# One 512-column product for both halves of the activations in the loops of the feed-forward stages

## The reference

```python
def _swiglu(x, w_in, w_out):
    gate, up = jnp.split(x @ w_in, 2, axis=-1)
    return (jax.nn.silu(gate) * up) @ w_out
...
def swiglu(h, wg, wu, wd):
    return (jax.nn.silu(h @ wg) * (h @ wu)) @ wd
...
    h = x
    for i in range(DEPTH):                       # DEPTH = 1
        h = h + 0.5 * _swiglu(_rmsnorm(h, ffn1_norm[i]), ffn1_w_in[i], ffn1_w_out[i])
...                                              # mix
        h = h + 0.5 * _swiglu(_rmsnorm(h, ffn2_norm[i]), ffn2_w_in[i], ffn2_w_out[i])
...                                              # ple
    return _rmsnorm(h, final_norm)
...
    for i in range(DEPTH_2):                     # DEPTH_2 = 2
        mod = c_act @ ada_w[i] + ada_b[i]
        sh1, sc1, g1, sh2, sc2, g2, sh3, sc3, g3 = jnp.split(mod, N_MOD, axis=-1)
        h = modulate(rms_norm(x, ln_ffn1[i]), sh1, sc1)
        x = x + 0.5 * g1[:, None, :] * swiglu(h, ffn1_wg[i], ffn1_wu[i], ffn1_wd[i])
...                                              # attn where i is 0, sgu where i is 1
        h = modulate(rms_norm(x, ln_ffn2[i]), sh3, sc3)
        x = x + 0.5 * g3[:, None, :] * swiglu(h, ffn2_wg[i], ffn2_wu[i], ffn2_wd[i])
        x = rms_norm(x, ln_out[i])
```

## Time and profile before

| | us |
|---|---|
| median of 3 runs | 1601.67 |
| lowest and highest | 1601.16, 1603.94 |
| the profiled execution's own time | 1601.59 |
| its span in the profile | 1599.8 |

### The profile page before, as it was taken

One profiled execution on the slowest core, in us unless ns is written; L12 is line 12 of the kernel. 1 busy time (PEld: TensorE's weight loads), 2 busy tenths in 40 slices (PEclk: granted clock), 3 DMA queues, 4 the chain that ended last, 5 costly groups with the idle time before them and its releaser, 6 DMA issues.

```text
span 1599.8 us, 30197 instructions
## 1 busy us (share of the span) xinstructions
PE 1550.6 (97%) x12438; PEld 1510.9 (94%) x12438; DVE 1116.6 (70%) x1327; ACT 740.1 (46%) x823; POOL 13.0 (1%) x33
## 2 busy tenths in 40 slices
PE   6999999799999999999999899999999999999998
PEld 6999998689999999999888799999999999899998
DVE  4777879956887867877767677788644466654444
ACT  5433354354333574333567643335533346453333
POOL 1000000000000000000000000000000000000000
PEclk8999999899999999999999999999999999999999
DMA  6998854238888448888443388885555554545551
GB/s 212 344 313 295 285 158 154 84 126 283 295 290 309 162 152 301 308 304 296 138 158 115 106 299 304 294 279 196 182 184 184 184 158 151 166 159 184 184 184 53
DMA packets 244682, 341.08 MB, mean 213 GB/s; under 512 B 5891, under 2 KB 188315, under 8 KB 244624
## 3 DMA queue, kind: packets, MB, share of 16 engines
q1 hardware_dynamic: 242656, 334.72, 62.4%
q0 software_dynamic: 1968, 5.54, 0.9%
HBM read 339.17 MB, written 2.63 MB: 214 GB/s over the span
## 4 chain that ended last, share of the span: by engine, by line
PE 89%; DVE 5%; ACT 4%; DMA 1%; issue 1%; SPq 0%; DVEq 0%; ACTq 0%
PE bank L1323 28%; PE bank L1325 28%; PE bank L1324 28%; ACT w_hi L447 1%; DVE w_lo L825 1%; PE bank L1451 1%; DVE arena L1042 1%; PE bank L1395 1%; ACT L467 1%; ACT xn L458 1%; DVE xn L976 1%; DMA raw<-in_ffn_w_in 1%; DVE x_res L993 1%; PE bank L1384 0%; PE bank L1663 0%
## 5 line engine op out<-in xcount | busy, mean ns | idle before, releaser
L1323 PE MATMUL bank<-xs_hi,w_hi 128*128 128x256 f32 x2496 | 714.1, 286 | 11.1 <-DVE xs_lo L831 8.5
L1325 PE MATMUL bank<-xs_hi,w_lo 128*128 128x256 f32 x2496 | 708.3, 284 | 0.0
L1324 PE MATMUL bank<-xs_lo,w_hi 128*128 128x256 f32 x2496 | 708.3, 284 | 0.0
L825 DVE TENSOR_TENSOR w_lo<-raw,w_hi 128x2048 fp32r<-128x2048 f32 x245 | 560.0, 2287 | 206.2 <-ACT w_hi L447 205.9
L447 ACT ACTIVATE w_hi<-raw 128x2048 fp32r<-128x2048 f32 x245 | 466.4, 1906 | 234.2 <-PE bank L1325 216.2
L1323 PEld LDWEIGHTS bank<-xs_hi,w_hi 128*128 128x128 f32 x2496 | 481.2, 193 | 18.9 <-issue 18.3
L1324 PEld LDWEIGHTS bank<-xs_lo,w_hi 128*128 128x128 f32 x2496 | 481.3, 193 | 1.3 <-issue 1.3
L1325 PEld LDWEIGHTS bank<-xs_hi,w_lo 128*128 128x128 f32 x2496 | 481.0, 193 | 0.0
L1323 PE MATMUL bank<-gu_hi,w_hi 128*128 128x256 f32 x960 | 274.6, 286 | 0.0
L1325 PE MATMUL bank<-gu_hi,w_lo 128*128 128x256 f32 x960 | 271.7, 283 | 0.0
L1324 PE MATMUL bank<-gu_lo,w_hi 128*128 128x256 f32 x960 | 271.6, 283 | 0.0
(11 more groups left out here) (236 smaller groups left out, 1205.0 us busy)
## 6 DMA issues: line engine op xcount, KB each, us to landing
ada<-in_ada_w SPq DMA_DIRECT2D x72, 1024.0 KB, 6.1
raw<-in_ffn_w_in SPq DMA_DIRECT2D x44, 1024.0 KB, 7.4
raw<-in_ffn_wg SPq DMA_DIRECT2D x44, 1024.0 KB, 5.5
raw<-in_ffn_wu SPq DMA_DIRECT2D x44, 1024.0 KB, 5.4
raw<-in_ffn_wd SPq DMA_DIRECT2D x44, 1024.0 KB, 5.0
raw<-in_ffn_w_out SPq DMA_DIRECT2D x22, 1024.0 KB, 6.7
raw<-in_attn_w_qkv SPq DMA_DIRECT2D x12, 1024.0 KB, 5.1
raw<-in_w_in SPq DMA_DIRECT2D x10, 1024.0 KB, 5.4
```

Source lines behind the costliest of these rows:

```text
L825: dve.tensor_tensor(w_lo[:, s, :], raw[:, s, :], w_hi[:, s, :].bitcast(F32), ALU.subtract)\
L1323: pe.matmul(out_, a_hi, b_hi, start=start, stop=False, skip_group_check=True)
L1324: pe.matmul(out_, a_hi, b_lo, start=False, stop=False, skip_group_check=True)
L1325: return pe.matmul(out_, a_lo, b_hi, start=False, stop=stop, skip_group_check=True)
```

## The change

1. `xs_hi` and `xs_lo` become the two halves of one tile `xs`. In the loops, gate and up go through `wide_halves`: the high weight streams high and low activations of a k-tile together as one product of 512 columns (256 columns each), and the low weight streams the 256 high ones into the left half of the same bank. Each half of the output now fills a bank of its own, so gate and up take two banks each: the gate takes also `MISC`, the up also `STAT`.
2. The left and right side of such a bank are added by one VectorE `tensor_reduce` (output 128x512 from 1024 inputs per partition; the two numbers that are added lie 256 apart): `gate_sum` to `silu_g`, and `gu_mul_of_sum` to `gu`, followed by the multiply, now from SBUF. ScalarE's silu reads and writes `silu_g`.
3. As `MISC` now holds half of the gate, the transposes of the ada sum wait for `gate_summed`, and TensorE waits for `ada_stored` at the end of each turn with ada.
4. Where a stage's first chunk waits k-tile by k-tile (in `wide`), the four products that need the high activations come first, behind a wait for `xhi_ready` or `cs_hi_ready`, and the two that need the low ones come behind a second wait. The attention's first chunk and the gating unit's keep their order.
5. In `projected` and at the end of attn, the first two `add_squares` come after the `split`, ahead of the last two additions to x, and the third comes last.

```diff
-        xs_hi = sb("xs_hi", [P, KT, T], F32R)
-        xs_lo = sb("xs_lo", [P, KT, T], F32R)
+        xs = sb("xs", [P, 2, KT, T], F32R)
+        xs_hi, xs_lo = xs[:, 0], xs[:, 1]
...
-        bank = [ctx.enter_context(nc.psum_tensor(f"bank{i}", [P, 2 * T], F32)) for i in range(8)]
+        banks8 = ctx.enter_context(nc.psum_tensor("banks8", [P, 8, 2 * T], F32))
+        bank = [banks8[:, i, :] for i in (0, 1, 2, 3, 4, 6, 5, 7)]
+        HALVES_GATE, HALVES_UP = (banks8[:, i:i + 2, :].rearrange("p a (h n) -> p a n h", h=2) for i in (4, 6))
...
+                def silu_of_sum(i):
+                    act.wait_ge(gate_summed, LOOPED * f + i + 1)
+                    act.activation(silu_g[:, :], silu_g[:, :], ACT.Silu).then_inc(silu_done, 1)
...
-                    silu(i + 2, cl + 3 * i)
+                    silu_of_sum(i)
...
+                def gate_sum(i):
+                    dve.wait_ge(chunks_done, cl + 3 * i + 1)
+                    dve.tensor_reduce(silu_g[:, :].rearrange("p (a n) -> p a n", a=2), HALVES_GATE, AX_X, ALU.add)\
+                        .then_inc(gate_summed, 1)
+
+                def gu_mul_of_sum(i):
+                    dve.wait_ge(chunks_done, cl + 3 * i + 2)
+                    dve.wait_ge(gulo_ready, s0 + 2 + i)
+                    dve.tensor_reduce(gu[:, :].rearrange("p (a n) -> p a n", a=2), HALVES_UP, AX_X, ALU.add)\
+                        .then_inc(up_summed, 1)
+                    dve.wait_ge(up_summed, LOOPED * f + i + 1)
+                    dve.wait_ge(silu_done, s0 + 3 + i)
+                    dve.tensor_tensor(gu[:, :], gu[:, :], silu_g[:, :], ALU.mult).then_inc(gu_ready, 1)
...
                     split((cl + 2, i), (cl + 2) % SLOTS)
+                    gate_sum(i)
                     if f < 4:
                         ada_half(i, 1)
                     split((cl + 3, i), (cl + 3) % SLOTS)
-                    gu_mul(i + 2, cl + 3 * i + 1)
+                    gu_mul_of_sum(i)
...
                 split(c + 4)
-                residual(n, done, ks=range(2, 6))
+                residual(n, done, ks=range(2, 6), adds=False)
                 split(c + 5)
-                residual(n, done, ks=range(6, KT))
+                for b in range(2):
+                    add_squares(n + 1, b)
+                residual(n, done, ks=range(6, KT), adds=False)
+                add_squares(n + 1, 2)
...
+                for k in range(KT) if each is not None else ():
+                    halves = [(bank[b][:, nb * T:(nb + 1) * T], slice(nb * P, (nb + 1) * P)) for nb in range(2)]
+                    pe.wait_ge(each[0], each[2] + k + 1)
+                    for nb, (o, m) in enumerate(halves):
+                        pe.matmul(o, wh[:, k, m], hi[:, k, :], start=(k == 0 and nb == 0), stop=False, skip_group_check=True)
+                        pe.matmul(o, wl[:, k, m], hi[:, k, :], start=False, stop=False, skip_group_check=True)
+                    pe.wait_ge(each[1], each[2] + k + 1)
+                    for o, m in halves:
+                        ins = pe.matmul(o, wh[:, k, m], lo[:, k, :], start=False, stop=(k == KT - 1), skip_group_check=True)
+                ins.then_inc(chunks_done, 1)
+
+            def wide_halves(s, b, pair):
+
+                wh, wl = lin(s, w_hi), lin(s, w_lo)
+                for nb in range(2):
+                    o = bank[b + 2 * nb]
+                    for k in range(KT):
+                        m = slice(nb * P, (nb + 1) * P)
+                        pe.matmul(o, wh[:, k, m], pair[:, :, k, :], start=(k == 0), stop=False, skip_group_check=True)
+                        ins = pe.matmul(o[:, 0:T], wl[:, k, m], pair[:, 0, k, :], start=False, stop=(k == KT - 1),
+                                        skip_group_check=True)
                 ins.then_inc(chunks_done, 1)
...
-                    wide(cl % SLOTS, GATE, xs_hi, xs_lo)
+                    wide_halves(cl % SLOTS, GATE, xs)
                     arrived(cl + 1, i)
                     pe.wait_ge(gu_ready, s0 + 2 + i)
-                    wide((cl + 1) % SLOTS, UP, xs_hi, xs_lo)
+                    wide_halves((cl + 1) % SLOTS, UP, xs)
...
                         pe.wait_ge(ada_step, 8 * LOOPED * f + 8 + 8 * i)
+                        pe.wait_ge(gate_summed, LOOPED * f + i + 1)
...
                     over_two((cl + 2) % SLOTS, *g_half, False, False, between=ada_sum if f < 4 else None)
+                    if f < 4:
+                        pe.wait_ge(ada_stored, LOOPED * f + i + 1)
```

More of the change, by code:

```diff
@@ L977, in add_squares, with residual @@
                         .then_inc(sq_added, 1)
-            def residual(n, done, banks=range(4), ks=range(KT)):
+            def residual(n, done, banks=range(4), ks=range(KT), adds=True):
                 kind = STAGES[n][0]
@@ L994, in residual @@
                                              op0=ALU.mult, op1=ALU.add).then_inc(x_ready, 1)
-                    if k % 2 == 0 and k > 1:
+                    if adds and k % 2 == 0 and k > 1:
                         add_squares(n + 1, k // 2 - 1)
@@ L1001, in projected @@
                 split(c + 3)
-                residual(n, done, ks=range(2))
+                residual(n, done, ks=range(2), adds=False)
                 split(c + 4)
-                residual(n, done, ks=range(2, 6))
+                residual(n, done, ks=range(2, 6), adds=False)
                 split(c + 5)
-                residual(n, done, ks=range(6, KT))
+                for b in range(2):
+                    add_squares(n + 1, b)
+                residual(n, done, ks=range(6, KT), adds=False)
+                add_squares(n + 1, 2)
             def modulation(layer):
@@ L1258, in attention @@
                 split(c + 15)
[L1259 removed]
+                residual(n, lambda b: (chunks_done, c + 12 + b + 1), OUT_BANK, range(6), False)
                 split(c + 16)
[L1261 removed]
+                for b in range(2):
+                    add_squares(n + 1, b)
+                residual(n, lambda b: (chunks_done, c + 12 + b + 1), OUT_BANK, range(6, KT), False)
+                add_squares(n + 1, 2)
                 split(c + 17)
@@ L1333, in wide @@
                 wh, wl = lin(s, w_hi), lin(s, w_lo)
-                order = [(k, nb) for nb in range(2) for k in range(KT)] if each is None else \
-                    [(k, nb) for k in range(KT) for nb in range(2)]
-                for k, nb in order:
-                    if each is not None and nb == 0:
-                        pe.wait_ge(each[0], each[1] + k + 1)
-                    ins = mm3(bank[b][:, nb * T:(nb + 1) * T], wh[:, k, nb * P:(nb + 1) * P],
-                              wl[:, k, nb * P:(nb + 1) * P], hi[:, k, :], lo[:, k, :],
-                              k == 0 and nb == 0, k == KT - 1)
+                if each is None:
+                    for k, nb in [(k, nb) for nb in range(2) for k in range(KT)]:
+                        ins = mm3(bank[b][:, nb * T:(nb + 1) * T], wh[:, k, nb * P:(nb + 1) * P],
+                                  wl[:, k, nb * P:(nb + 1) * P], hi[:, k, :], lo[:, k, :],
+                                  k == 0 and nb == 0, k == KT - 1)
```

16 lines of the change are left out of this document (8 added, 8 removed).

## The result

The changed kernel takes 1581.5 us (median of 4 runs, 1580.8 to 1582.9) against 1601.4 for the kernel before: a ratio of 0.988, 95% interval 0.9865 to 0.9891. It is faster by 19.9 us, where 32.4 were forecast. The time lies inside the range 1546 to 1594, but 12.5 us above the predicted 1569 and 1.5 above the 1561 to 1580 that the forecast's own reading was given. The profiled execution took 1580.8 us with a span of 1579.0, so 20.8 us are gone from the span.

A forecast was written before the change was run, and what follows sets the result against it. The prediction took the loops, 54 turns, as bound by TensorE alone. Gains of 23.0 (products), 7.8 (ends) and 3.6 (starts) less 2.0 of costs made 32.4 us, from 1601.6 to 1569 us; own range 1561 to 1580, wider range 1546 to 1594.

The forecast's parts named there:

- the forecast's own reading: Loops' gate and up: 13.3 ns go with each product whatever its length; forecast 1569 us, chance 0.50.
- Products: Loops' gate and up: a pair takes 346.7 ns instead of 360, over 1728 pairs a gain of 23.0 us.
- load was the excess: Rival, loops: 512 columns hide the weight load, a pair takes 336 ns, gain 41.5 us, total 1551 us; chance 0.22.
- columns are what costs: Rival, loops: float32r columns are slower, a pair stays at 360 ns, only ends and starts gain, 1592 us; chance 0.15.
- The forecast's one sign of a product free of its 13 ns: Line 1325: shortest record 274 ns against median 283, read as most of the 13 ns not being the price of columns.
- The estimate by TensorE: Loops: by the skill page, three products take 327 ns and the new two 325, some 4 us in all.
- Reductions: Loops, VectorE: two sums of 1.22 us add 2.44 us a turn, 16.7 of 17.29 us with ada, still hidden.
- the rival that would have made the kernel slower: VectorE becomes the bound in turns with ada, at 2.28 us a reduction: 1624 us; chance 0.10.
- Costs of the first turn and the modulation: TensorE waits 1.5 us for `ada_store` in the first layer's first turn, plus 0.5 us for two layers with modulation; between 0 and 4.
- Ends: Ends of mix, attn, sgu: the split leaves the chain, gaining 2.5, 1.5 and 3.8 us, together 7.8, between 4 and 9.
- the clock did what was said: End of sgu: with TensorE's idle time cut from 2.6 to 1 us, square sums run at granted clock 1.00.
- Starts: First chunks of five ffn layers, mix, ple and sgu's output: 0.45 us each, 3.6 us, between 0 and 5.

The follow-up runs named there:

- the turned pair: Changed kernel with one gate pair per loop turn in reversed order (256-column product first, then 512): 1571.1 us, ratio 0.9811 to the kernel before.
- the products alone: Not the model: rows of 96 products of each shape on TensorE alone, four rows again with VectorE and ScalarE working; 512 float32r columns took 227 ns.
- e5: Changed kernel with the pairs of every other k-tile turned round in the loops (high, low, low, high): 1572.8 us, ratio 0.9822 to the kernel before.
- the ends' part: Kernel before plus only high-part products first and square sums after the residuals, loops as before: 1591.9 us, ratio 0.9946.
- either part alone: Two runs on the kernel before: only wide gate and up products with VectorE sums, 1590.6 us; only the reordered starts and ends, 1591.9 us.

## Why the prediction came out as it did

**Products: the mechanism was right, the size was not.** The step was "13.3 ns go with each product and its weight load, whatever its length. The pair takes 213.3 + 13.3 + 120 = 346.7 ns". Alone on the engine all of it holds: 227, 173 and 120 ns, and the pair 346.7. In the loops, behind 48 products of 256 columns, TensorE fell into the slower of two rhythms at 353.3 ns, and stayed there in 53 of 54 turns. 6.7 ns x 1728 = 11.5 us are the gap in the loops, and nearly all of the 12.5 by which the forecast missed; the turned pair gave 10.4 of them back. What went wrong was to add up prices of products as if a price didn't depend on the sequence. From the kernel's time alone the forecast would not have been told from its rival: 353.3 lies halfway between 346.7 and 360, and it is the products alone and the turned pair that decide. The rivals "load was the excess" (336) and "columns are what costs" (360) are refuted by the products alone (512 columns take 227 ns, not 216 and not 240). The forecast's one sign of a product free of its 13 ns was misread: records of 274 ns belong to a rhythm, and the same records stand in the pairs that do pay it twice. The estimate by TensorE: Matmul & The Clock Gate of the Trainium skill (Back-to-back issue gap), N/2.4 + 2.5 ns, agrees with the BF16 rows (109 and 216) and not with float32r (120 and 227). Why the second turn ran fast is shown in part. A late start can be such a seam, but isn't always: in the run with the sum done twice 29 turns start late (328 to 332 ns from the first product to the next), and 17 of them ran at 346.7 and 12 at 353.3, while all 25 that start on time ran at 353.3; the second turn of the kernel with the halves beside each other started late too and ran at 353.3. What decides it, and why a seam of 384 or a turned pair moves TensorE and others don't, is open.

**Reductions: right.** 1219 and 1218 ns against 1.22 us:

```profile
L888 DVE TENSOR_REDUCE silu_g<-banks x54: 1216/1219/1225, 60.0 to 1552.5; 128x512 f32<-128x1024 f32 x54
...
L894 DVE TENSOR_REDUCE gu<-banks x54: 1217/1218/1221, 66.3 to 1558.4; 128x512 f32<-128x1024 f32 x54
```

Pairs 256 apart in PSUM cost nothing over the line through the earlier trace rows. VectorE did not become the bound; the rival that would have made the kernel slower needed 1.5 us a sum, and the sum done twice shows it at work (2.5 us for the gate: 0.43 us late a turn).

**Costs of the first turn and the modulation: the places right, the sizes not, and one place more.** The forecast had TensorE wait 1.5 us for `ada_store` behind the first turn. VectorE's `ada_store` and TensorE's seam between first and second turn in the changed kernel:

```profile
68.30 0.68 DVE L927 TENSOR_REDUCE mod<-banks 128x512 f32 x1
```

```profile
69.20 0.28 PE L1353 MATMUL banks<-gu_hi,w_lo 128*128 128x256 f32 x1
69.62 0.49 PE L1386 MATMUL banks<-xs,w_hi 128*128 128x512 f32 x1
```

The second turn starts 0.64 us behind the end of `ada_store`, 0.3 us late, and its next product another 0.1. In the run with the sum done twice all 29 late turns start 0.60 to 0.66 us behind it, and in no trace does a turn start closer. So it is the wait of the forecast, 0.4 us instead of 1.5. The 0.5 us for two layers are there too, but once in each: behind the second and fourth layer's last turn TensorE's next product comes 0.47 us late, waiting for the last `gu_lo` (533.42 to 534.01 us in the second), and the one behind it 0.07. Together some 1.5 us of the 2.0. A place that the forecast did not have is the wait ahead of the first transposes, for the ada sum. The changed kernel's profile has none, but all eight whole-kernel experiments show one, of 0.2 to 2.5 us, here the turned pair's kernel, its waits of TensorE between 50 and 72 us:

```profile
PE banks L1501 <- DVE ada_acc L919: 2.0, 1, 2.0
```

In the trace of e5 the chain goes from there back to the landing of the first ada weights at 56.5 us. Why the wait is 2.5 us in one profile and nothing in another, these runs don't tell; it stands in the run of the ends' part as well (0.7), so the faster gate and up chunks alone don't make it.

**Ends: the place right, some 1.1 us too much.** The chain no longer goes through the split. The end of mix in the changed kernel, to be set beside the earlier trace rows: PE's timeline at the last product and the first sums, then the chain that ended last.

```profile
342.10 0.28 PE L1353 MATMUL banks<-cs_hi,w_lo 128*128 128x256 f32 x1
342.22 0.59 PE L1440 MATMUL banks<-xn,ones_d 128*128 128x256 f32 x2
```

```profile
342.42 0.76 DVE x_res L1015 x2
343.17 0.34 DVE xn L998
343.51 0.04 issue
343.56 1.58 PE banks L1440 x6
```

Forecast: the additions of k-tiles 6 and 7 start 0.2 us behind the start of the first square sum, 2.5 us earlier than before. They do (342.22 and 342.42). But before, only the addition of k-tile 7 stood behind the split; now both stand there, 0.76 us. From the start of the first square sum to the end of the last, before and now, mix went from 5.11 to 2.92 us, attention (to the scaling of x) from 5.07 to 4.02, spatial gating from 6.45 to 3.05: 2.2, 1.05 and 3.4 where 2.5, 1.5 and 3.8 were forecast, together 6.65 instead of 7.8. In spatial gating the clock did what was said. Windows of the six sums before and of the additions and sums now:

```profile
1394.20:1397.10 2.90, 2.87 (x7) 2.34 (x8) 0.37 (x1) 0.51 (x2) 0.00 (x0) 0.53 0.78 267
```

```profile
1375.80:1378.70 2.90, 2.46 (x12) 1.85 (x11) 1.21 (x3) 0.81 (x2) 0.00 (x0) 1.00 0.81 328
```

A granted clock of 0.53 (the 1.2 GHz level for most of it, after 2.6 us with TensorE idle) became 1.00 (the 2.4 GHz level): the sums take 1.58 us instead of 2.85.

**Starts: right in sum, and in part by luck.** The trace of the ends' part alone is 10.3 us shorter than the kernel's before; without the 6.65 of the ends 3.7 remain, forecast 3.6 (by the medians, 9.2 us apart, 2.6 remain). By place, from one stage's first square sum to the next one's and without the ends: mix and the third, fourth and sixth feed-forward layers gain 0.34 to 0.49 us, as forecast; ple, the fifth layer and spatial gating, at 0.45 each in the forecast, gain nothing; and the first layer, at nothing in the forecast, gains 0.7 and the second 1.0. Why, no run shows.

**The sum again**, with what was measured: 11.5 + 6.65 + 3.7 = 21.9, and the span shrank by 20.8. Against it stand the costs of 1.5 us and 0.5 us in attention that only some profiles show, 2.0 us where 1.1 are missing; the rest is less than the first layer varies by from profile to profile. In attention the granted clock of the changed kernel is below the one before:

```profile
885.00:902.00 17.00, 14.20 (x99) 13.34 (x99) 9.97 (x15) 11.00 (x14) 0.00 (x0) 0.90 0.20 63
```

Before it was 1.00 from 885 to 905, as in the traces of either part alone. Its cause is open.

## What to carry to other kernels

The price of a product is one of a sequence: before adding up prices, look at the nanoseconds between starts for a period, and compare turns of the same loop, since one odd turn can show a faster state that the code can be brought into. Such a state can hang on the order of two instructions; try it on the engine alone, where a dozen seams fit into one run, and then in the kernel. Where two versions are too close for their times, compare the traces stage by stage. And where a cheaper product hands work to another engine, read that engine's need from the window of the tightest turn, and prove the slack by doing the new work twice.

## What the hardware showed

- Float32r products cost columns/2.4 + 13.3 ns at the full clock from 256 columns up (120, 173, 227 ns), against 109 and 216 ns in BF16; 128 columns take 111 ns against 56.
- Products of 512 and 256 columns in turn run at 346.7 or 353.3 ns a pair, for as long as the sequence goes on. Behind 256- or 512-column products it is 353.3; one turned pair, two and two, a lone 384 or some cuts bring it to 346.7, and so did 96 products of 128 columns ahead. In the kernel's loop a late start did so in 17 of 29 turns. Mirrored throughout it is 348.3.
- Where the pair's two parts lie in memory (beside each other or 8 KB apart) makes no difference.
- VectorE sums 512 pairs that lie 256 apart in PSUM in 1219 ns, which is where 1024 inputs stand on the line between the 691 ns for 512 and the 2277 ns for 2048 of the earlier trace rows.
- In a loop whose TensorE turn ends with a wait, the next turn's first product started 0.60 to 0.66 us behind the end of the VectorE sum waited for, in turns where nothing else was later.
